# The samples' columns by one matmul, the attention one unit later, and x scaled by the matmul that turns it

## What is computed

```python
def token_mixer(x, ...):
    h = rms_norm(x, norm1_w)
    z = h @ w_in
    ...
    y_conv = (zb * y_c) @ w_conv_out
    ...
    o = diff_attn(q, k, v, pos, pos, lam)          # samples: over the paged cache
    o = rms_norm(o, subln_w) * (1.0 - lam_init)
    y_diff = o.reshape(B, T, V_W) @ w_diff_out
    y_mem = mem_attn(qm, mem_k, mem_v).reshape(B, T, CROSS_W) @ w_cross_out
    g = jax.nn.sigmoid(zg.reshape(B, T, N_BRANCH, D_MODEL))
    merged = g[:, :, 0] * y_conv + g[:, :, 1] * y_diff + g[:, :, 2] * y_mem
    return x + merged @ w_o, ...
```

## Time and profile before

| | |
|---|---|
| runs | 2852.84, 2854.64, 2857.38 us; median 2854.64 |
| the profiled execution | 2857.79 us, its span 2855.9 us |
| busy | PE 87%, PEld 56%, DVE 49%, ACT 12%, POOL 36% |
| chain that ended last | PE 53%, DMA 25%, DVE 12%, issue 5%, POOL 4% |
| granted TensorE clock, mean | 0.964 |

### The profile page before, as it was taken

How to read it: one execution, slowest core, us unless ns; L and a number is a source line. 1 busy time by engine, 2 the same in 40 slices (tenths; PEclk the granted TensorE clock), 3 DMA queues, 4 the chain that set the end, 5 groups by cost and what they waited for, 6 DMA issues and landing times.

```text
span 2855.9 us, 28287 instructions
## 1 busy us (share of the span) xinstructions
PE 2478.5 (87%) x9241; PEld 1592.3 (56%) x9241; DVE 1390.6 (49%) x2168; ACT 355.1 (12%) x760; POOL 1038.9 (36%) x952
## 2 busy tenths in 40 slices
PE   6899999979999999999998687777899587777777
PEld 4777788868766668888776333232333133223333
DVE  2365566862112213000057687876555655556543
ACT  2111000012221111000120211101011011111010
POOL 1165566020122210000015556556445443555442
PEclk9999999989999999999999899999899889999999
DMA  5499999594598975443459999999999989999999
GB/s 156 153 335 319 316 337 335 192 332 153 195 339 322 330 275 180 155 138 119 146 200 355 401 421 417 417 417 411 422 422 416 413 360 422 418 421 417 421 422 376
DMA packets 305393, 913.67 MB, mean 320 GB/s; under 512 B 15634, under 2 KB 195946, under 8 KB 236652
## 3 DMA queue, kind: packets, MB, share of 16 engines
q0 software_dynamic: 122304, 723.48, 63.0%
q1 hardware_dynamic: 182980, 188.92, 20.3%
HBM read 905.80 MB, written 6.56 MB: 319 GB/s over the span
## 4 chain that ended last, share of the span: by engine, by line
PE 53%; DMA 25%; DVE 12%; issue 5%; POOL 4%; ACT 1%; DVEq 0%; POOLq 0%; ACTq 0%; SPq 0%
PE ps L573 20%; PE ps L651 12%; DMA sb_S<-in_peer_u_dram,sb_ring 10%; DMA sb_bregion<-in_peer_u_dram,sb_ring 6%; PE ps L663 6%; PE ps L878 4%; DMA sb_mkv<-in_peer_u_dram,sb_ring 3%; PE ps L641 3%; PE ps L751 2%; DVE sb_bregion L1765 2%; DMA sb_wring<-in_w_in_dram 2%; DVE sb_S L1765 2%; DMA sb_S<-in_peer_v_dram,sb_ring 1%; POOL sb_bregion L486 1%; POOL sb_wring L486 1%
## 5 line engine op out<-in xcount | busy, mean ns | idle before, releaser
L878 PE MATMUL ps<-sb_wring,sb_ring 128*128 128x512 f32 x992 | 462.7, 617 | 129.7 <-DMA sb_wring<-in_peer_v_dram,sb_ring 80.8
L573 PE MATMUL ps<-sb_hT,sb_wring 128*128 128x264 f32 x2304 | 533.4, 393 | 18.2 <-DMA sb_wring<-in_w_peer_q_dram 8.7
L573 PEld LDWEIGHTS ps<-sb_hT,sb_wring 128*128 128x128 f32 x2304 | 442.2, 193 | 101.5 <-issue 23.1
L878 PEld LDWEIGHTS ps<-sb_wring,sb_ring 128*128 128x128 f32 x992 | 189.0, 197 | 404.2 <-issue 270.4
L1765 DVE CUSTOM_DVE_ANT_0 sb_bregion<-sb_bregion,sb_rows 128x2048 f32<-128x2048 f32 x128 | 293.6, 2294 | 228.7 <-DMA sb_bregion<-in_peer_u_dram,sb_ring 221.6
L651 PE MATMUL ps<-sb_hT,sb_wring 128*128 128x264 f32 x1536 | 365.8, 389 | 9.2 <-issue 6.8
L651 PEld LDWEIGHTS ps<-sb_hT,sb_wring 128*128 128x128 f32 x1536 | 286.5, 190 | 74.8 <-issue 27.7
L486 POOL DMA_INDIRECT sb_bregion<-in_peer_u_dram,sb_ring x132 | 187.2, 1419 | 280.2 <-DVEq L1183 228.0
L878 PE MATMUL ps<-sb_hT,sb_ring 128*128 128x512 f32 x496 | 234.9, 623 | 46.2 <-DMA sb_hT<-in_peer_v_dram,sb_ring 35.0
L878 PE MATMUL ps<-sb_oreg,sb_ring 128*128 128x512 f32 x496 | 223.4, 597 | 39.8 <-DMA sb_oreg<-in_peer_v_dram,sb_ring 37.2
L1150 ACT ACTIVATE sb_ring<-sb_ident,sb_ring 128x128 f32<-128x128 f32 x248 | 99.6, 402 | 909.5 <-PE ps L878 702.1
(11 more groups left out here) (349 smaller groups left out, 2530.2 us busy)
## 6 DMA issues: line engine op xcount, KB each, us to landing
sb_wring<-in_w_in_dram SPq DMA_DIRECT2D x52, 2048.0 KB, 13.3
sb_ring<-in_cache_k_dram POOLq DMA_DIRECT2D x64, 512.0 KB, 6.5
sb_mkv<-in_cache_k_dram POOLq DMA_DIRECT2D x64, 512.0 KB, 6.8
sb_mkv<-in_cache_v_dram POOLq DMA_DIRECT2D x48, 512.0 KB, 6.9
sb_rows<-in_cache_v_dram POOLq DMA_DIRECT2D x47, 512.0 KB, 7.0
sb_wring<-in_w_mem_kv_dram SPq DMA_DIRECT2D x8, 2048.0 KB, 8.8
sb_wring<-in_w_o_dram SPq DMA_DIRECT2D x8, 2048.0 KB, 8.1
sb_wring<-in_w_peer_q_dram SPq DMA_DIRECT2D x8, 2048.0 KB, 13.7
```

The lines of the kernel that those rows point to most:

```text
L573: last = mm(ps[:, (2 * r + c) % 4, 0:NT], wring[:, r, k, c * P:(c + 1) * P], rhs[:, k, :], start=(k == 0), stop=(k == KC - 1))
L878: last = mm(ps[:, 4 * t + q, :], diag[:, k % 4, :], e_slots[v % ER][:, q * 512:(q + 1) * 512], start=False, stop=q_stop, skip_group_check= ...
```

## The change

1. Opening: VectorE squares x as its first work. The factors no longer multiply x's rows; they multiply three identity tiles (`small`), and TensorE's transposes become matmuls with those tiles. `cols` and `stT` are copied after that, the lambda products after the last block of `hT`. ScalarE's exponential of lambda moves behind the second root.
2. Units: softmax steps and attention move a unit later, and `first_unit(a)` is 2a + 2; units 0 and 1 have no work between their matmuls up to (1, 23). The branch chunk of unit 1 goes to PSUM bank 5, so it need not wait for `first_merge(0)`.
3. Samples' values: after masking, VectorE adds the heads' parts together (`own_sum`, 256 numbers in a row for the memory and 128 for the pages), and `columns` turns them by two matmuls or one, in place of eight.

```diff
+        head_rows, halves, half_rows = stat[:, 48:48 + HEADS], stat[:, 56:58], stat[:, 32:40]
+        own_sum = mq_w[:, :]
...
-            pe.wait_ge(s["x_scaled"], 2)
+            pe.wait_ge(s["x_scaled"], 1)
             for k in range(KC):
+                if k < 2:
+                    pe.wait_ge(s["cols_ready"], 1)
...
-                transpose_rows(x_rows, k, k % 8, TILES).then_inc(s["xT_full"], 1)
+                for t, (first, n) in enumerate(TILES):
+                    last = mm(ps[:, k % 8, first:first + n], x_rows[0:n, t, k * P:(k + 1) * P], small[0:n, t, 0:n], start=True, stop=True)
+                last.then_inc(s["xT_full"], 1)
...
-                pe.wait_ge(s["y_taken"], q + 2)
+                pe.wait_ge(s["y_taken"], q + 2 if bank == 2 else 2)
...
-                pick = halves if m < MEM_ROUNDS else ones[:, 0:1]
-                n = pick.shape[1]
-                for h in range(BC):
-                    last = mm(ps[:, (q + 1) % 2, NT + h * n:NT + (h + 1) * n], own_heads[:, h * P:(h + 1) * P], pick, start=True, stop=True)
+                pick, parts = (half_rows, 2) if m < MEM_ROUNDS else (head_rows, 1)
+                for f in range(parts):
+                    last = mm(ps[:, (q + 1) % 2, NT + 8 * f:NT + 8 * f + 8], own_sum[:, f * P:(f + 1) * P], pick, start=True, stop=True)
...
-                if (q, k) == (0, 15):
+                if (q, k) == (1, 23):
                     turn_maxima(0, nk)
-                if (q, k) == (0, 23):
+                if (q, k) == (2, 7):
                     spread_maxima(0, nk)
-                if (q, k) == (1, 23):
+                if (q, k) == (3, 4):
                     sum_partitions(0, nk)
...
-                a = (q - 1) // 2
+                a = (q - 2) // 2
...
                       head_rows[:, 0:heads].unsqueeze(2).broadcast_to([P, heads, DC // heads]), ALU.mult))
+                st(RED(own_sum[:, 0:DC // heads], own_heads.rearrange("p (h c) -> p c h", h=heads), X, ALU.add))
                 signal("sums_masked")
...
-                if a < ATTN and q % 2:
+                if a < ATTN and q % 2 == 0:
...
                     maxima_of(a)
                     normalise(a)
```

More of the change, by code:

```diff
@@ L645, in _, with gate_chunk @@
             own_scores()
-            def gate_chunk(b, r, c, q, operand, landed, between=None, ready=None):
+            def gate_chunk(b, r, c, q, operand, landed, between=None, ready=None, bank=2):
                 pe.wait_ge(s["gate_done"], q + 1)
@@ L662, in gate_chunk @@
                 for k in range(BC):
-                    last = mm(ps[:, 2, 0:NT], bwring[:, r, k, c * P:(c + 1) * P], operand[:, k, :], start=(k == 0), stop=(k == BC - 1))
+                    last = mm(ps[:, bank, 0:NT], bwring[:, r, k, c * P:(c + 1) * P], operand[:, k, :], start=(k == 0), stop=(k == BC - 1))
                     if k == BC - 1:
@@ L1222, in _ @@
             row_factors(1, stat[:, 0:3])
-            signal("x_ss2")
-            for t in (0, 2):
-                n = TILES[t][1]
-                st.run(TSC(x_rows[0:n, t, :], x_rows[0:n, t, :], stat[0:n, t:t + 1], None, ALU.mult))
+            dve.wait_ge(s["consts"], 1)
+            for t, (_, n) in enumerate(TILES):
+                st.run(TSC(small[0:n, t, 0:n], ident[0:n, 0:n], stat[0:n, t:t + 1], None, ALU.mult))
             st.settle()
             signal("x_scaled")
-            dve.wait_ge(s["cols_ready"], 1)
+            dve.wait_ge(s["cols_full"], 1)
+            st.run(CP(cols[:, :], ps[:, 0, 0:72]))
+            dve.wait_ge(s["st_full"], 1)
+            st(CP(stT[:, :, :], ps[:, 1, 0:P].rearrange("p (a b) -> p a b", a=BC)))
+            signal("cols_ready")
             for k in range(1, KC, 2):
@@ L1233, in _ @@
                 signal("xT_taken2")
+            dve.wait_ge(s["lam_in"], 64)
+            st(TT(lam4[:, 0, :], lam4[:, 0, :], lam4[:, 1, :], ALU.mult))
+            st(TT(lam4[:, 2, :], lam4[:, 2, :], lam4[:, 3, :], ALU.mult))
+            st(RED(lam[:, 0:1], lam4[:, 0, :], X, ALU.add))
+            st(RED(lam[:, 1:2], lam4[:, 2, :], X, ALU.add))
+            signal("lam_pre")
             row_factors(2, stat[:, 3:5])
@@ L1552, in keep_columns @@
                 if m < MEM_ROUNDS:
-                    st(CP(oT_mem[:, :, TP + 2 * m:TP + 2 * m + 2], ps[:, (q + 1) % 2, NT:NT + 2 * BC].rearrange("p (h b) -> p h b", b=2)))
+                    for f in range(2):
+                        st.run(CP(oT_mem[:, f:BC:2, TP + 2 * m:TP + 2 * m + 2], ps[:, (q + 1) % 2, NT + 8 * f:NT + 8 * f + 8].rearrange("p (b h) -> p h b", b=2)))
+                    st.settle()
                 else:
@@ L1583, in _ @@
             st(TT(head_rows, head_rows, ident[:, 3 * QUAD:3 * QUAD + HEADS], ALU.add))
+            for f in range(2):
+                st.run(TSC(half_rows[:, MH * f:MH * f + MH], head_rows[:, 0:MH], halves[:, f:f + 1], None, ALU.mult))
+            st.settle()
             own_maxima()
+            first_merge(0)
             turned_maxima(0, P)
-            first_merge(0)
+            first_merge(1)
             exponents()
@@ L1597, in _ @@
             normalise(1)
-            first_merge(3)
+            first_merge(4)
             memory_sums()
             weights()
-            first_merge(4)
-            for q in range(5, 32):
-                a = (q - 1) // 2
+            first_merge(5)
+            for q in range(6, 32):
+                a = (q - 2) // 2
                 if 8 <= q < 12:
```

75 lines of the change are left out of this document (31 added, 44 removed).

## The result

| | before | after |
|---|---|---|
| median, runs beside each other | 2856.76 us (5 runs) | 2833.35 us (5 runs, 2829.35 to 2840.59) |
| ratio to before, 95% interval | | 0.9918 [0.9898, 0.9939] |
| the profiled execution | 2857.79 us | 2829.35 us, span 2827.7 us |
| granted TensorE clock, mean | 0.964 | 0.965 |

The change gains 23.4 us by the medians. The forecast was 2815.5 with a range to 2832; the measured median lies 1.4 us outside it, on the slow side. That 1.4 us is inside the noise (the interval of the ratio stands for a gain of 17 to 29 us), but the forecast gain of 39.4 us is not: the sign was right and the size was not. The profiled execution is the fastest of its five, so its 28.4 us are more than the change is worth.

A forecast was written before the change was run, and what follows sets the result against it. TensorE, nearly always busy in the unit stage, was taken as the bound, with transfers a possible second. Terms 6.0 + 14.6 + 16.8 + 6.2 − 4.2 = 39.4 us off 2854.64 gave a median of 2815.5, range 2806 to 2832.

The forecast's parts named there:

- A: Opening: TensorE starts 6.7 us earlier, blocks dearer, clock rises after 5 us: gain 6.0 us, lower bound −2.6.
- R1: Rival: the clock stays at half in the opening, blocks take 22.5 us, gain 30.8, time 2824; chance 0.2.
- B: First softmax wait of TensorE: 17.70 us shrinks to 3.7, plus 0.6 for the clock: gain 14.6 us.
- C: Columns of the samples' values: 32 matmul instructions instead of 192, 3.6 us instead of 20.4: gain 16.8 us.
- D: TensorE's waits at unit starts: nine, 7.8 us, fall to two, 1.6 us: gain 6.2 us.
- E: VectorE's new sum takes 1.9 us, so TensorE waits 0.5 in each of 8 units: loss 4.2 us.
- the room of 1.35 to 1.4 us: Time after the masking, read in unit 13, that the new sum may take before TensorE's value round waits.
- R2: Rival: the sum with jumps of 128 costs 3.6 us, TensorE waits 2.25 per odd unit; 2829; chance 0.12.
- R3: Rival: transfers become the bound at 335 GB/s in the value units; gain 30.4, time 2824; chance 0.12.
- R4: Rival: slower than before, everything from the value round on waits for a sum of 5.2 to 6.8 us; chance 0.02.
- R5: Rival: the softmax wait moves instead of shrinking, as VectorE's merges come first; gain there 12.5; no chance of its own.

The follow-up runs named there:

- the shift alone: Kernel before with only softmax and attention moved a unit later, opening and eight-matmul columns as before: 2830.50 us, ratio 0.9917.
- the run that waits for the mask: Changed kernel, but value rounds wait for the masking alone and only the columns wait for the new sum: 2823.66 us, ratio 0.9886.

## Why the prediction was wrong

**A. Opening: forecast +6.0, measured about −3.6** (mean first gate unit 605.5 against 601.9). This step failed twice. The start at 21.1 was right. The cost of a block was reckoned "by columns", 1.4 us at the lower clock and 0.95 at the full; it was 1.68, since a turning costs by the instruction (or by the load that goes with it), 8 columns as much as 128. And the clock was let rise after 5 us, from one place where 264-column matmuls followed transposes; it stayed at its lower level for all 27 us. The first fault was in reach: 48 instructions in 13.19 us, one in three of them with 8 rows, are 0.275 each, and 96 of them 26.4 us. Rival R1 had the clock right and the block wrong (22.5 us). Its lower bound of −2.6 was no bound: at the first chunk the loss is 6.5 us, from the 26.8 us of the blocks.

**B. First softmax wait: forecast +14.6, measured +15.0** ("g to v", 125.0 to 110.0). That the two are so close is luck. The wait left is 5.8, not 3.7, since VectorE's keys ended 2.2 us later in that execution: 2.1 us less. And 2.6 us more come from attention work that went behind the first value round, which the forecast did not see.

**C. Columns: +16.8 forecast, 17.7 measured** (16.1 in "v to w" and 1.6 behind it). **D. Unit starts: +6.2 forecast, 5.4 measured** in the shift alone, 8.0 without the 2.6 that came over from B. The waits themselves did as forecast, two of 0.8 are left; where the other 1.8 us come from is open. B and D together, which the border does not touch, are 20.4 against 20.8.

**E. The new sum: −4.2 forecast, −10.2 measured** (the gain of the run that waits for the mask). The price of the sum was right to 0.02 us, taken from the row with jumps. The step that failed is the room of 1.35 to 1.4 us, in two pieces. It was read in unit 13 and taken for all eight rounds, while five of them stand behind a merge of two instructions: 0.47 us less room, there already in the kernel before. In the last of these TensorE also came 0.44 us sooner. And the shift, another part of the same change, puts the attention's last step ahead of the merge: 0.50 us less again in most units. I had looked in the new order for where the attention's steps had left, and not for where they had gone. So TensorE's round starts late, against before, by 0.47, 1.16 and 1.06 us in the first three of the eight, by 1.51 in the next four and by 1.94 in the last, 10.7 by the timeline, where 0.5 each was forecast.

**The sum.** −3.6 + 15.0 + 11.4 ("v to w", C, D and E together) + 1.6 (the last columns) = 24.4, against 23.4 and 22.8 measured. The forecast's 39.4 is over by 9.6 in A and by 5.8 in C to E (18.8 against 13.0), and under by 0.4 in B. Its median has a slip as well: 2854.64 less 39.4 is 2815.2, not 2815.5.

**The rivals.** R1 happened. R2 (a sum of 3.6 us) did not, but its price was too low: it gave 2829, and the sum made twice, 3.8 us, took 2864. R3 (transfers) is excluded by the run that waits for the mask. R4 was held a distant case, at 5.2 to 6.8 us of sum; the sum made twice, 3.8 us, is already slower than before, because the gain to be eaten was 34 (23.4 + 10.2) and not 44, the room was smaller, and the lower clock adds about 1.6 for each wait. R5 did not show.

**The range.** It combined no two rivals. A at −3.6 and E at −10.2 together leave 23.8 of gain by its other terms, near 2831: each alone was inside the range, and the two of them put the time at its edge.

## To carry to other kernels

Where small matmuls replace transposes, count instructions, not columns, take the price of one from the transposes that they replace, and ask at which clock that price was read. When a change both adds work to an engine and reorders that engine, take the slack for the added work from the new order, in more than one unit: read who stands ahead of it there. A release that only the first of two steps gives should be signalled between them; that one moved line was worth 10 us here. Waits of 1.2 us for the sum left the clock at 1.00, waits of 2.3 us and more did not.

## What was not expected of the hardware

- Float32 matmul instructions with 8 moving columns and a stationary operand of 128 columns took 0.213 us each at the lower clock, when repeated (6.83 us for 32), the same as the distance between the starts of two with 128 moving columns there (0.21).
- The clock stayed at its lower level through 26.8 us of gapless matmuls with 128 and 8 moving columns. In the 264-column matmuls after them, which start at 49.06, the distance between two starts falls from 0.44 us to 0.22 at 53.1.
- The 16 late blocks of transposes, the same code in all twelve profiled kernels, took 8.4 us in three of them, at a clock of 1.00, and 11.5 to 12.9 in the other nine, where it fell to 0.50 within 3 us of their start. No code explains the difference.
- VectorE pays for jumps about alike on the reading and on the writing side: 1.90 and 2.01 us for 1024 numbers against 1.22.
